# Filler matmuls in front of six waits of TensorE

## The reference

```
first block:
  n    = rmsnorm(x) ; proj = n @ w_in           # 1024 -> q,k,v,gates,z,xbc,dt
  o    = [gated linear attention | Mamba-2 SSD] # chunked scans
  h    = x + o @ w_out
  h    = h + peer(rmsnorm(h))                   # 16384 single-neuron experts, top 16 of 8 heads
  x    = rmsnorm(h)
second block:
  layer 0: uv = gelu(rms(h) @ a_w_in); v = layer_norm(v)
           m  = (u * (W_s v + b)) @ a_w_out ; h += rms(m) ; h += rms(relu(h' @ up)^2 @ down)
  layer 1: K, V from h; q = rms(h) @ w_q; chunked band attention, 16 heads
           h += rms(o @ w_o) ; h += rms(relu(h' @ up)^2 @ down)
```

## Time and profile before

| what | value |
|---|---|
| median of 3 runs | 2759.64 us (2756.28 to 2759.88) |
| the profiled execution | 2760.13 us, span 2758.4 us |
| TensorE busy | 2635.8 us (96% of the span), 14417 matmul records |
| VectorE, ScalarE, GpSimd busy | 66%, 38%, 34% |
| mean granted clock of TensorE | 0.982 |

### The profile page before, as it was taken

How to read it: one execution, slowest core, us unless ns; L and a number is a source line. 1 busy time by engine, 2 the same in 40 slices (tenths; PEclk the granted TensorE clock), 3 DMA queues, 4 the chain that set the end, 5 groups by cost and what they waited for, 6 DMA issues and landing times.

```text
span 2758.4 us, 37590 instructions
## 1 busy us (share of the span) xinstructions
PE 2635.8 (96%) x14417; PEld 2371.7 (86%) x14417; DVE 1824.0 (66%) x3139; ACT 1044.2 (38%) x1695; POOL 946.5 (34%) x532
## 2 busy tenths in 40 slices
PE   8799999899999999999999899999999989999998
PEld 6668899899999999999999877888889756888887
DVE  5644799988888878888888645670735055590542
ACT  5333334345555543333333343422223254522221
POOL 2323410014444442333333135344442422344442
PEclk9899999999999999999999899999999999999999
DMA  3222236569999988999999422233331321233331
GB/s 132 92 84 71 91 107 190 158 194 309 347 346 351 329 309 299 350 348 337 344 350 346 137 91 84 77 98 94 97 95 62 107 84 54 70 109 97 95 97 54
DMA packets 235473, 488.47 MB, mean 177 GB/s; under 512 B 85128, under 2 KB 135192, under 8 KB 235040
## 3 DMA queue, kind: packets, MB, share of 16 engines
q1 hardware_dynamic: 198432, 351.83, 39.8%
q0 software_dynamic: 36864, 134.23, 13.4%
HBM read 442.98 MB, written 42.88 MB: 176 GB/s over the span
## 4 chain that ended last, share of the span: by engine, by line
PE 81%; DVE 14%; ACT 2%; issue 1%; DMA 1%; POOL 0%; SPq 0%; DVEq 0%; ACTq 0%
PE ps L293 25%; PE ps L294 24%; PE ps L295 24%; PE ps L1644 3%; DVE wl L282 2%; PE ps L462 1%; DVE ti L1504 1%; DVE ti L1499 1%; DVE hT L2167 1%; PE ps L2410 1%; DVE tv L1502 1%; PE ps L2495 1%; DVE oh L1590 1%; DVE slot L1602 1%; DVE sR L1500 1%
## 5 line engine op out<-in xcount | busy, mean ns | idle before, releaser
L274 ACT ACTIVATE wh<-wraw 128x1024 fp32r<-128x1024 f32 x487 | 513.1, 1058 | 1291.5 <-PE ps L295 1287.3
L293 PE MATMUL ps<-Xh,wh 128*128 128x512 f32 (+2 forms) x2312 | 864.9, 374 | 40.3 <-DVE wl L282 12.8
L282 POOL TENSOR_TENSOR wl<-wraw,wh 128x1024 fp32r<-128x1024 f32 x231 | 562.1, 2438 | 946.5 <-ACT wh L274 946.5
L294 PE MATMUL ps<-Xl,wh 128*128 128x512 f32 (+2 forms) x2312 | 822.5, 356 | 0.0
L295 PE MATMUL ps<-Xh,wl 128*128 128x512 f32 (+2 forms) x2312 | 820.9, 355 | 0.0
L293 PEld LDWEIGHTS ps<-Xh,wh 128*128 128x128 f32 x2312 | 442.9, 192 | 87.9 <-issue 19.5
L294 PEld LDWEIGHTS ps<-Xl,wh 128*128 128x128 f32 x2312 | 443.5, 192 | 38.0
L295 PEld LDWEIGHTS ps<-Xh,wl 128*128 128x128 f32 x2312 | 441.2, 191 | 40.6
L282 DVE TENSOR_TENSOR wl<-wraw,wh 128x1024 fp32r<-128x1024 f32 x256 | 312.3, 1221 | 141.7 <-ACT wh L274 141.6
L293 PE MATMUL ps<-Hh,wh 128*128 128x384 f32 x1024 | 346.6, 338 | 8.0 <-DVE Hl L1854 8.0
L294 PE MATMUL ps<-Hl,wh 128*128 128x384 f32 x1024 | 345.6, 337 | 0.0
(11 more groups left out here) (307 smaller groups left out, 3353.9 us busy)
## 6 DMA issues: line engine op xcount, KB each, us to landing
wraw<-in_uT SPq DMA_DIRECT2D x128, 512.0 KB, 5.1
wraw<-in_v SPq DMA_DIRECT2D x128, 512.0 KB, 5.5
wraw<-in_up SPq DMA_DIRECT2D x128, 512.0 KB, 3.6
gA_scratch<-gl SPq DMA_DIRECT2D x122, 192.0 KB, 5.6
gl<-gA_scratch SPq DMA_DIRECT2D x122, 192.0 KB, 5.4
gG_scratch<-gbuf SPq DMA_DIRECT2D x64, 256.0 KB, 7.8
lg<-gG_scratch SPq DMA_DIRECT2D x128, 128.0 KB, 5.4
wraw<-in_w_q SPq DMA_DIRECT2D x24, 512.0 KB, 3.6
```

Of the source, the lines that this page charges most:

```text
L274: act.activation(wh[:, n % 4, :], wraw[:, n % 4, :], ACT.Copy).then_inc(s_wh, 1)
L282: pool.tensor_tensor(wl[:, n % 4, :], wraw[:, n % 4, :], wh[:, n % 4, :].bitcast(F32), ALU.subtract).then_inc(s_wl, 1)
L293: pe.matmul(o, ah, bh, start=start, stop=False)
L294: pe.matmul(o, ah, bl, start=False, stop=False)
```

## The change

A helper multiplies `ones` by itself n times into a bank, each time with start and stop set, behind a wait that the bank is free. It is called at six places. At the first, the wait for the constant `ones` moves ahead of the first projection. In `last_sums_pe` the wait that the bank is free comes with the helper, ahead of the wait for s_sd. At the other four the helper stands ahead of the waits that were there.

```diff
+    def keep_busy(pe, b, n):
+        bank_free(pe, b)
+        for _ in range(n):
+            pe.matmul(ps[b][:, 0:128], ones[:, :], ones[:, :], start=True, stop=True)
...
     def last_sums_pe(pe):
         b = AUX["acl"]
+        keep_busy(pe, b, 45)
         pe.wait_ge(s_sd, 2)
-        bank_free(pe, b)
...
+        pe.wait_ge(s_const, C_ONES)
+        keep_busy(pe, 7, 30)
         pe_linear(pe, IN_A, [0, 1, 2], B_INA, XL["in"], done, first=(0, 1, 2))
-        pe.wait_ge(s_const, C_ONES)
         root_pe(pe, "in", 5)
...
     def gating_pe(pe, g):
         b = 5 + g % 3
         if g == 0:
+            keep_busy(pe, b, 22)
             pe.wait_ge(s_ws, 1)
             pe.wait_ge(s_ln, 20)
...
     def gmlp_pe(pe):
+        keep_busy(pe, 5, 16)
         pe_linear_tok(pe, A_V, 0, B_TOK[0], XL["av"], lambda tc: (s_vn, tc + 1))
...
         gating_pe(pe, 7)
+        keep_busy(pe, 7, 10)
         pe_linear(pe, A_O, list(range(6)), B_AO, XL["ao"], lambda g: (s_mo, g + 1), first=(0, 1, 2))
...
+        keep_busy(pe, 4, 18)
         query(0)
```

## The result

| | before | after |
|---|---|---|
| median of 10 runs each | 2756.20 us (2750.96 to 2763.20) | 2762.15 us (2756.67 to 2767.59) |
| the profiled execution, span | 2760.13, 2758.4 us | 2759.20, 2757.5 us |
| mean granted clock | 0.982 | 0.985 |

What follows compares the result with a forecast made beforehand. TensorE, whose chain ended last for 81% of the span, was taken as the bound. Site terms -2.7 + 0 - 2.2 + 4.9 + 0 - 1.1 gave -1.1 us: 2759.0 us for the profiled execution, median 2758.5, range 2752 to 2765.5.

Steps and rivals of the forecast that it cites:

- Site 4: 22 fillers before the first gating: start only after the wait, when bank 5 is released, so plain added work, +4.9 us.
- Site 1: 30 fillers before the first projection: done before the weights arrive, projection begins at full clock, -2.7 us.
- Site 2: 45 fillers before the last sums: 4.8 us idle remains behind them, the clock falls again, 0 us.
- Rival (c): The 45 fillers before the last sums keep the clock: -3.1 us in all, 2756.5 us; chance 8%.
- Site 3: 16 fillers before the gMLP's first V projection: end 0.2 us late, projection runs at full clock, -2.2 us.
- so this is passed on as well: At the first V projection: its 2.4 us gain reaches VectorE's layer norm chain, which begins only when the projection is done.
- 8.4 low fillers: Before the first V projection: 8.4 of 16 fillers run at low clock, 7.6 at full, done at 1580.0 us.
- rival (a): Fillers don't raise the clock or let it fall, 0.44 us each: sum +21.4 us, 2781 us; chance 7%.
- Site 6: 18 fillers before the first query: 1.7 us idle before them keeps the clock, 1.8 back less 0.65 late, -1.1 us.
- Site 5: 10 fillers before the A_O projection: they end inside the wait, the clock was already full there, 0 us.
- (b): Bank 5 is free earlier, so the first gating's fillers lie inside its wait: -2.1 there, sum -8.1, 2751.5 us; chance 7%.
- Rival (d): Leads lost: absorbed at first projection (2761.2 us), clock low at first query (2760.7), or both (2763.4); chance 18%.

Runs made afterwards that it cites:

- the fillers inside the waits: Kernel before plus fillers before first projection (30), last sums (64), first gating (26, bank 6) and first query (20, bank 0): 2748.28 us, ratio 0.9970.

## Why the prediction was wrong

**Site 4, right.** Forecast +4.9. The fillers started behind the copy that releases bank 5, not inside the wait; +4.9 between the medians without and with it, +4.5 to +5.0 net in the segments. The size is a net one: the fillers took 7.3 us, being low for 4.87 of them, and the work behind them, now at full clock, gave 2.3 back. Reading `bank_free` against the last reader of that bank, and that reader against who ended the wait, was enough.

**Site 1, right in kind, too large.** Forecast -2.7, measured 2.2 by traces and 1.7 by times (ratio 0.9994, whose interval reaches zero). The term mis-sized is the low start: 5.77 us in the first trace of before, 4.58 in the mean of nine traces.

**Site 2, right.** 90 records in 10.21 us at full clock, then 4.84 us idle and 5.65 us at 0.50 behind it. Forecast 0, ratio 0.9999. Rival (c) is refuted for 45 fillers and has its price, 2.0 us, with 64.

**Site 3, the first step that failed.** Forecast -2.2. At the site it is right in all seven traces, -2.0 to -2.3: the fillers fill the wait, and the V projection behind them runs at full clock. The step "so this is passed on as well" failed. (Its count of 8.4 low fillers should be 7.7 by its own 0.44 us, and rival (a)'s +1.9 there 2.1; both change the sum by 0.2 us at most.) The shorter half-projection is followed by the root's one-column matmuls and a wait of half a microsecond, and there the clock now falls: +1.6 us in six of seven. Net by these two, where the fall comes: about -0.5. A fall at 2106 us, +2.8 to +3.1 in three of the seven and none of the others, makes more of it. The times have +4 alone (0.3 to 7.7) and nothing in company.

**Site 6, the second.** Forecast -1.1. The idle gap of 1.78 us kept the clock in all six traces with bank 4, and -1.08 to -1.12 arrived at the first query. The step that failed is the one that books the kept clock as a gain of the whole kernel. It is repaid at 2378 us: a gap of 1.99 us, some 165 us later, with full clock behind it in the three traces of before, is now followed by a low stretch (+1.5 to +1.7), and the end is 0.33 later. Net +0.8; ratio of site 6 alone 1.0001. The Trainium skill, page "TensorE: Matmul & The Clock Gate", section "Why this matters for your kernels", warns of idle gaps between bursts of matmuls, and only of ones longer than this. The trace doesn't agree: a fall followed this gap of 1.99 us in nine of ten traces with site 6, and in one of eight without, so the length of the gap alone doesn't settle it.

**Site 5.** Forecast 0, and no time shows more. The traces do: with site 4 and without site 5 the clock fell behind this wait (+1.9 us, two traces of two), and with both sites it falls neither there nor near 1741 us (-1.5). I saw neither: my sum asked of each site only what its own wait does.

**The sum.** By the segments: site 4 +4.9, site 1 -2.2, site 2 0, site 5 -1.5, site 6 +0.8, site 3 -0.5. That is +1.5, and 5.5 (3 to 8) was measured. With site 3's +4 from its time alone it would be +6.0. So forecast and result lie 6.6 us apart, and the segments account for 2.6 of them: 0.5 at site 1, 1.7 at site 3, 1.9 at site 6, less the 1.5 that came unforeseen with site 5. What makes up the rest stays open. Two candidates are seen and not tested: the longer stretch at 2106 us, 1.3 us in the mean of the traces with site 3, and the row from 102.5 to 1573.4 us, where traces with site 2 are longer. Rival (a) is refuted by the pace of the first 30 fillers, (b) by the wait that stands in front of L296. Rival (d) was nearest, and its 2761.2 to 2763.4 us hold the measured time, but by luck: leads were lost, only not where it looked (absorbed at site 1, or low at site 6), rather further on. The prediction took falls that come in one execution and not in the next as noise of 3 us either way; the counts above show that some of them go with the change.

**Left open.** Why the fall near 2378 us comes with nearly any kernel that has site 6, whatever bank its fillers use, and why those near 1600 and 1741 us go with sites 3 and with 4 and 5. Why site 3 costs 4 us alone and nothing beside the others; its interval allows 0.3. Why the fillers inside the waits gain the full sum. And single events that no edit here explains: the stretch near 264 us in four traces of eighteen, and 5.4 us lost between 915 and 1000 us in the kernel without site 4. The latter isn't mainly the clock: it has one low stretch of 3.4 us, and between 905 and 935 us ScalarE waits 11.1 us in 3 times for the DMA of weight tiles, longest 4.8, a wait that no other trace has there.

## What to carry to other kernels

Fillers on a matrix of ones did hold TensorE's clock here, and they gained where they lay wholly inside a wait: look up who last read their bank and when, and leave little idle time behind them (0.57 us kept the clock here, 4.84 didn't). In front of a wait that is ended by that same last reader they are plain work on the critical path. Don't book a kept clock as its share of one low stretch: look at every later gap of about 2 us and every run of tiny matmuls, since with the fillers other ones of them were followed by a fall, and time the whole in many runs.

## What the runs showed of the hardware

I had not expected that fillers at one place go with falls of the clock at places tens or hundreds of microseconds further on, and fairly regularly: 1600 us with site 3 (six of seven traces against none of eleven), 2378 us with site 6 (nine of ten against one of eight), and none at 1741 us with sites 4 and 5 (none of six against twelve of twelve). The same gap, 1.99 to 2.01 us at the same moment of the program, was followed by 0.50 in one kernel and by 1.00 in the other. Work that kept TensorE busy in the records, 10 records in 3.41 us at 1600 us, ran at 0.50 behind a stretch of one-column matmuls. A 128x128 float32 matmul of ones took 0.225 us at full clock and 0.42 us at the low one. Fillers beside VectorE's chain cost it nothing: the stretch from 39.9 to 85.2 us kept its length to 0.04 us in all kernels, with 0, 45 or 64 of them. And a single execution of the kernel before can be off by 5 us (2750.96 to 2763.20 around 2756.20), as much as this whole change.
